# Matmuls of zeros put into TensorE's idle time at the LayerNorm boundaries of a two-part transformer block

## The chip, the cores and the metric

The kernel runs on one core of one Trainium2 chip. A core has TensorE (PE in the profile, with PEld for its weight loads), VectorE (DVE), ScalarE (ACT), GpSimd (POOL) and SyncE (SP, which here only issues DMAs). The metric is the device time of one execution in microseconds; lower is better.

## The reference

One sequence of 256 tokens with 1024 features passes through two blocks of two layers each. What surrounds the change is the first block:

```python
h = layer_norm(x, ln_in_g, ln_in_b)
for l in range(DEPTH):                       # DEPTH = 2
    proj = h @ w_in[l]                       # 1024 -> 1888
    ...                                      # conv branch, GQA, gated spatial unit, MLA
    mix = jnp.concatenate([o_a, o_b, o_c, o_d], axis=-1) @ w_out[l]
    h = layer_norm(DEEPNORM_ALPHA * h + mix, ln_mix_g[l], ln_mix_b[l])
    up = depthwise_conv(h @ ffn_w_up[l], ffn_conv_w[l], ffn_conv_b[l])
    f = (jax.nn.silu(up[..., :D_FF]) * up[..., D_FF:]) @ ffn_w_down[l]
    h = layer_norm(DEEPNORM_ALPHA * h + f, ln_ffn_g[l], ln_ffn_b[l])
```

The second block has four feed-forward parts, a state-space mixer, a sliding-window attention and two cross-attentions, each behind an RMS norm. All numbers are float32.

## The kernel before, in words

The program is written by hand, one instruction stream for each engine, with semaphores between them; each stream runs in the order in which its code stands. A list of phases (`phases()`) is the same for all engines: start, then for each layer of the first block `mixer`, `norm("mix", l)`, `convffn`, `norm("ffn", l)`, and then the second block.

Matmuls are made from split operands: a float32 number is a high part in a short format plus a low remainder, and three products (high by high, low by high, high by low; `PASSES`) stand for one. Weights come in units of 1 MB by DMA into a ring of three slots (`raw`); ACT writes the high parts (`w_hi`, L1193), DVE the low parts (`w_lo`, L1655). `feature_major` (L639) makes 128 output features by 256 tokens from 8 blocks of 128 input features: 24 matmuls of 256 columns. Two such halves are one weight unit (`pair_fm`, or `up_pair` in the feed-forward), so two units are 96 matmuls.

A LayerNorm boundary of the first block goes like this. The last projection before it adds into PSUM banks 4 to 7: banks 4 and 5 are the first 128 tokens (`tt` = 0), 6 and 7 the second 128. DVE adds them to the stream `x` (L1652), takes the statistics (L1730, L1732), ACT the square root (L1285), and DVE writes the centred and scaled rows to `z`, which lies in the tensor `mix` (L1738), and signals `z_ready` once for each `tt`. PE then transposes them in `turn` (L677), 8 blocks of 128x128 for each `tt`, into banks 0 to 3. ACT applies gain and bias to two blocks for each bank (L1221) and signals `xhi_ready`, four times in all. DVE has one piece of work between: the low part of a weight unit (L1655, 128x2048). Then, for each of the four banks, DVE writes `xt_hi` (L1718) and `xt_lo` (L1655) and signals `bank_drained`. The first matmul of the next phase (`stream_tile`, inside `feature_major`) waits for the first of these four parts, the matmuls of blocks 2, 4 and 6 for the others. POOL meanwhile makes the new `x` from `z` (L2298, L2299) with operations on the same 1024 columns.

`zero` is a tensor of 512 columns of bfloat16 zeros. Before the change it is used once in each feed-forward part: four matmuls of one row by 512 columns (L786) clear banks 4 to 7.

In the second block a boundary is an RMS norm; its `turn` is the same function.

Of the kernel before, what the change touches and what calls it, by code (L numbers as in the profile page):

```python
# [28 lines left out]
P = 128  # L29
# [253 lines left out]
def mixed_block_kernel(nc, inp, consts, mem_dram, out, upto=None):  # L283
# [6 lines left out]
    with ExitStack() as ctx:  # L290
        def sb(name, shape, dt=F32):
            return ctx.enter_context(nc.sbuf_tensor(name, shape, dt))

        def sem(name):
            return ctx.enter_context(nc.semaphore(name))

        bank = [ctx.enter_context(nc.psum_tensor(f"bank{b}", [P, HALF], F32)) for b in range(8)]
# [10 lines left out]
        mix = sb("mix", [P, 2 * KT, T])  # L308
        xt_raw = mix[:, 0:KT, :]
        z = mix[:, KT:2 * KT, :].rearrange("p (t a) b -> p t (a b)", t=TT)  # L310
# [14 lines left out]
        zero = sb("zero", [P, HALF], mybir.dt.bfloat16)  # L325
# [116 lines left out]
        xhi_ready = sem("xhi_ready")  # L442
# [56 lines left out]
        RESIDUAL = {("mix_norm_2", l): (f"ffn1.{l}", 0.5) for l in range(2)}  # L499
# [84 lines left out]
        def _(pe):  # L584
            seen = Count()
            mm = pe.matmul

            def claim(b, name):

                n = names.claim(b, name)  # L590
                if n >= 2:
                    pe.wait_ge(bank_drained[b], n - 1)
                return bank[b]

            def taken(name):

                b, n = names.of[name]
                pe.wait_ge(bank_drained[b], n)
# [53 lines left out]
            def pair_fm(unit, b, name):  # L652

                w = weights(unit, (KT, 256))
                dst = claim(b, name)
                first = First()
                for j in range(2):
                    ins = feature_major(dst[:, T * j:T * j + T], w, P * j, P, first)
                ins.then_inc(bank_full[b], 1)

            def pair_tm(unit, b, name):

                w = weights(unit, (KT, 256))
                dst = claim(b, name)
                first = First()
                for tt in range(TT):
                    ins = token_major(dst[:, 256 * tt:256 * tt + 256], w, tt, 0, 256, first)
                ins.then_inc(bank_full[b], 1)

            def turn(src, tag):  # L670

                for b in range(4):
                    claim(b, f"{tag}.t{b}")
                for tt in range(TT):
                    pe.wait_ge(z_ready, seen.next(z_ready))
                    for k in range(KT):
                        ins = pe.transpose(bank[k // 2][:, T * (k % 2) + P * tt:T * (k % 2) + P * tt + P],  # L677
                                           src[:, tt, P * k:P * k + P], ident)
                        if tt == TT - 1 and k % 2:
                            ins.then_inc(bank_full[k // 2], 1)  # L680

            def turned(tag):

                assert not stream_due
                stream_due.extend((2 * b, f"{tag}.t{b}") for b in range(4))
# [30 lines left out]
            def start():  # L716
                pe.wait_ge(ident_in, 16)
                pe.wait_ge(ready, 1)

                def turn_parameters(b, first, groups):  # L720
                    claim(b, f"par{first}")
                    for i, g in enumerate(groups):
                        ins = pe.transpose(bank[b][:, P * i:P * i + P], stage[:, g, :], ident)
                    ins.then_inc(bank_full[b], 1)

                pe.wait_ge(early_in, 16 * EARLY_DMAS)
                turn_parameters(0, 0, range(1))
                turn(memx, "mem")
                turned("mem")
                for j in range(4):  # L730
                    pair_fm(f"mem{j}", j % 2, f"memk{j}")
                for j in range(4):
                    pair_tm(f"mem{4 + j}", 2 + j % 2, f"memv{j}")
                    if j == 0:
                        pe.wait_ge(const_in, 16)
                    if j < 3:
                        mean_squares("mem", x_sq, j)
                pe.wait_ge(stage_in, 16 * STAGE_DMAS)
                turn_parameters(0, 1, range(1, 5))
                turn_parameters(1, 5, range(5, ngroups))  # L740
                mean_squares("mem", x_sq, 3)
                turn(z, "x0")

            def mean_squares(tag, sq, h):

                pe.wait_ge(sq_ready, seen.next(sq_ready))
                b = 4 + h % 2
                claim(b, f"{tag}.ms{h}")
                for c in range(2):
                    ins = mm(bank[b][:, 0:T], cst("mean256"), sq[:, 2 * h + c, :], start=c == 0, stop=c == 1)  # L750
                ins.then_inc(bank_full[b], 1)

            def norm(tag, l):
                if (tag, l) != ("ffn", 1):
                    turn(z, f"{tag}{l}")

            def ffn_any(tag, prev):

# [396 lines left out]
            def xattn(l):  # L1155
                turned(f"xattn_norm_2{l}")

                for j in range(4):
                    pair_fm(f"xq{l}.{j}", j % 2, f"xq{l}.{j}")
                    if j >= 1:  # L1160
# [4 lines left out]
                out_rows([f"xo{l}.{j}" for j in range(4)], f"xo{l}")  # L1165

            run(dict(start=start, mixer=mixer, norm=norm, convffn=convffn, ffn=ffn, ssd=ssd, swa=swa,
                     xattn=xattn, store=lambda: None))

# [461 lines left out]
        def _(dve):  # L1631
# [39 lines left out]
            def split():  # L1671

                q = split_next[0]
                split_next[0] += 1
                slot, _, _, n = split_waits(q)
                dve.wait_ge(hi_ready, q + 1)
                tt_(w_lo[:, q % RING, 0:n], raw[:, slot, 0:n], w_hi[:, q % RING, 0:n].bitcast(F32),
                    ALU.subtract).then_inc(unit_split, 1)
# [728 lines left out]
        def _(sp):  # L2407
# [63 lines left out]
            def stream_ffn(tag, w_up, w_down):  # L2471
                up = w_up.rearrange("(k p) n -> p k n", p=P)
                down = w_down.rearrange("(r p) n -> p r n", p=P)
                _, s0, _, q0 = place[f"{tag}.gate0"]
                columns(f"{tag}.gate0", w_up, 0, 256)
                columns(f"{tag}.up0", w_up, DFF, 256)

                def load(k, i, dst_rows, src):
                    s = (s0 + k) % RING
                    sp.wait_ge(unit_split, q0 + k - RING + 1 if i is None else i * 6 + q0 + k - RING + 1)  # L2480
                    sp.dma_start(raw[:, s, :].rearrange("p (a b) -> p a b", a=dst_rows), src).then_inc(landed[s], 16)

                with sp.Fori(0, TURNS, 1) as i:
                    for c in (1, 2):
                        k = 2 + 3 * (c - 1)
                        load(k, i, KT, up[:, :, bass.ds(i * 512 + 256 * c, 256)])
                        load(k + 1, i, KT, up[:, :, bass.ds(i * 512 + DFF + 256 * c, 256)])
                        load(k + 2, i, 2, down[:, bass.ds(i * 4 + 2 * (c - 1), 2), :])
                rows(f"{tag}.down{NCHUNK - 1}", w_down, CHUNK_F * (NCHUNK - 1))
# [74 lines left out]
```

## Time and profile before

| | us |
|---|---|
| median of 3 runs | 2071.95 |
| lowest, highest | 2069.97, 2077.83 |
| span of the profiled execution (all that is listed of its time) | 2080.7 |
| mean granted TensorE clock in it | 0.933 |
| PE busy | 1932.7 (93%) |
| DVE busy | 1285.5 (62%) |
| ACT busy | 892.0 (43%) |

The profile is one execution. The share of PE in the chain of work that ended last is 84%, of DVE 10%. The granted clock is a share of TensorE's full rate; it has two values in this trace, 1.00 (2.4 GHz) and 0.50 (1.2 GHz). In the views by window the columns are the stretch, its length, the busy time of each engine with the number of its instructions, the clock, and DMA. In the timeline the columns are start, duration, engine, line and operation, operands, shapes, count, and in brackets the idle time before with what ended it.

### The profile page before, as it was taken

What the parts mean: (1) busy time and instruction counts of PE and PEld (TensorE: products, weight loads), DVE (VectorE), ACT (ScalarE), POOL (GpSimd) and SP (SyncE); (2) the same over time, 40 slices, a digit from 0 to 9 for tenths busy, and PEclk for the clock granted to TensorE, in tenths of its full rate; (3) what the DMA queues carried; (4) which work ended last, traced back from release to release, by engine and by line L of the source; (5) the groups of instructions that cost most, each with busy time, mean ns of one, the idle gap of its engine ahead of it and who ended that gap; (6) DMA issues with size and microseconds to landing.
All of it is one profiled execution on the core that took longest, in us unless ns stands there. A gap on an engine that the chain in (4) does not pass through costs nothing.

```text
span 2080.7 us, 31025 instructions
## 1 busy us (share of the span) xinstructions
PE 1932.7 (93%) x12412; PEld 1724.3 (83%) x12412; DVE 1285.5 (62%) x1559; ACT 892.0 (43%) x1076; POOL 101.8 (5%) x79
## 2 busy tenths in 40 slices
PE   7989799978979997999988999999999988999999
PEld 7966699976679997998986788999899875688998
DVE  5786877777687776555646556555555557565555
ACT  5444444434444443334543354333433444444332
POOL 0300200020020000000041000000000000000000
PEclk9987899988889998999986999999999995899999
DMA  9531355542135554555531434555455430224553
GB/s 299 186 111 50 134 182 181 183 133 102 61 122 182 188 189 131 185 190 168 161 105 61 142 142 151 189 185 181 162 182 182 164 119 21 100 87 160 187 189 126
DMA packets 226642, 310.78 MB, mean 149 GB/s; under 512 B 6598, under 2 KB 199398, under 8 KB 225926
## 3 DMA queue, kind: packets, MB, share of 16 engines
q1 hardware_dynamic: 223750, 298.06, 42.4%
q0 software_dynamic: 2528, 10.14, 1.5%
q10 hardware_dynamic: 288, 1.52, 0.2%
q8 instruction: 53, 0.87, 0.2%
q14 instruction: 23, 0.19, 0.0%
HBM read 306.56 MB, written 3.15 MB: 149 GB/s over the span
## 4 chain that ended last, share of the span: by engine, by line
PE 84%; DVE 10%; ACT 3%; issue 1%; POOL 1%; DMA 0%; DVEq 0%; ACTq 0%
PE bank L639 47%; PE bank L799 17%; PE bank L709 7%; PE bank L648 3%; PE bank L864 2%; PE bank L836 2%; DVE w_lo L1655 2%; DVE work L1652 1%; DVE x L1652 1%; PE bank L850 1%; DVE work L1655 1%; ACT mix L1303 1%; PE bank L1108 1%; ACT w_hi L1193 1%; DVE work L2231 1%
## 5 line engine op out<-in xcount | busy, mean ns | idle before, releaser
L1655 DVE TENSOR_TENSOR w_lo<-raw,w_hi 128x2048 fp32r<-128x2048 f32 x280 | 646.3, 2312 | 513.2 <-ACT w_hi L1193 513.0
L1193 ACT ACTIVATE w_hi<-raw 128x2048 fp32r<-128x2048 f32 x280 | 533.2, 1905 | 813.0 <-PE bank L639 532.4
L639 PE MATMUL bank<-xt_hi,w_hi 128*128 128x256 f32 x2752 | 791.8, 288 | 37.0 <-DVE xt_lo L1655 24.9
L639 PE MATMUL bank<-xt_lo,w_hi 128*128 128x256 f32 x2752 | 785.8, 286 | 0.0
L639 PE MATMUL bank<-xt_hi,w_lo 128*128 128x256 f32 x2752 | 785.4, 285 | 0.0
L639 PEld LDWEIGHTS bank<-xt_hi,w_hi 128*128 128x128 f32 x2752 | 535.4, 195 | 47.0 <-DVE xt_lo L1655 17.0
L639 PEld LDWEIGHTS bank<-xt_lo,w_hi 128*128 128x128 f32 x2752 | 535.3, 195 | 3.1 <-issue 0.7
L639 PEld LDWEIGHTS bank<-xt_hi,w_lo 128*128 128x128 f32 x2752 | 534.9, 194 | 0.0
L799 PE MATMUL bank<-w_hi,act_hi 128*128 128x512 f32 x528 | 206.4, 391 | 0.0
L799 PE MATMUL bank<-w_lo,act_hi 128*128 128x512 f32 x528 | 206.2, 390 | 0.0
L799 PE MATMUL bank<-w_hi,act_lo 128*128 128x512 f32 x528 | 205.4, 389 | 0.0
L799 PEld LDWEIGHTS bank<-w_hi,act_lo 128*128 128x128 f32 x528 | 99.1, 188 | 21.1
L799 PEld LDWEIGHTS bank<-w_hi,act_hi 128*128 128x128 f32 x528 | 99.4, 188 | 19.8 <-DVE act_lo L1655 0.9
L799 PEld LDWEIGHTS bank<-w_lo,act_hi 128*128 128x128 f32 x528 | 99.4, 188 | 18.3
L1652 DVE SCALAR_TENSOR_TENSOR work<-bank,par,work 128x255 f32<-128x255 f32 (+2 forms) x212 | 92.4, 478 | 25.7 <-ACT work L1342 18.4
L1193 ACT ACTIVATE work<-bank 128x512 f32<-128x512 f32 (+6 forms) x96 | 51.5, 545 | 117.0 <-PE bank L850 56.3
L709 PE MATMUL bank<-w_hi,act_hi 128*128 128x512 f32 x224 | 89.5, 399 | 6.7 <-ACT work L1475 3.0
L709 PE MATMUL bank<-w_lo,act_hi 128*128 128x512 f32 x224 | 88.8, 397 | 0.0
L709 PE MATMUL bank<-w_hi,act_lo 128*128 128x512 f32 x224 | 88.7, 396 | 0.0
L836 PE MATMUL bank<-work 128*128 128x256 f32 (+3 forms) x192 | 64.5, 509 | 19.9 <-DVE work L1655 9.1
L1342 ACT ACTIVATE work<-bank,par 128x256 f32<-128x256 f32 x88 | 44.5, 555 | 64.6 <-PE bank L639 64.6
L677 PE MATMUL bank<-con,mix 128*128 128x128 f32 x192 | 34.2, 341 | 40.4 <-DVE mix L1824 26.0
(256 smaller groups left out, 1874.0 us busy)
## 6 DMA issues: line engine op xcount, KB each, us to landing
raw<-in_ffn_wi SPq DMA_DIRECT2D x88, 1024.0 KB, 5.0
raw<-in_ffn_w_up SPq DMA_DIRECT2D x44, 1024.0 KB, 5.1
raw<-in_ffn_wo SPq DMA_DIRECT2D x44, 1024.0 KB, 4.8
raw<-in_ffn_w_down SPq DMA_DIRECT2D x22, 1024.0 KB, 5.3
raw<-in_w_in SPq DMA_DIRECT2D x14, 1024.0 KB, 5.3
raw<-in_ssd_in_proj SPq DMA_DIRECT2D x14, 1024.0 KB, 5.1
raw<-in_mem_wkv SPq DMA_DIRECT2D x9, 1024.0 KB, 8.4
raw<-in_w_out SPq DMA_DIRECT2D x8, 1024.0 KB, 5.0
```

The source lines that it names most:

```text
L639: ins = first(mm(dst, w[s][:, k, c0:c0 + m], xt[v][:, k, :], start=k == 0 and p == 0, stop=k == KT - 1 and p == 2))
L648: ins = first(mm(dst, xt[s][:, k, P * tt:P * tt + P], w[v][:, k, c0:c0 + n], start=start and k == 0 and p == 0, stop=k == KT - 1 and p == 2))
L677: ins = pe.transpose(bank[k // 2][:, T * (k % 2) + P * tt:T * (k % 2) + P * tt + P], src[:, tt, P * k:P * k + P], ident)
L709: ins = first(mm(bank[b][:, :], act[s][:, u % 2, r, P * tt:P * tt + P], w[v][:, r, HALF * h:HALF * h + HALF], start=u == 0 and r == 0 and ...
L799: ins = first(mm(bank[b][:, :], act[s][:, c % 2, j, P * tt:P * tt + P], w[v][:, j, HALF * h:HALF * h + HALF], start=False, stop=True, skip ...
L836: ins = mm(bank[b][:, at:at + n], d["q"][t][c], d["k"][c][:, 0:n], start=c == 0, stop=c == len(d["k"]) - 1)
L850: ins = pe.transpose(bank[b][:, dst:dst + P], prob[:, h % prob.shape[1], d["at"][t] + P * s:d["at"][t] + P * s + P], ident)
L864: ins = mm(bank[b][r:r + m, T * c + q0:T * c + T], v[s], prob_t[:, h % 2, T * s:T * s + T - q0], start=s == 0, stop=s == TT - 1 or d["keys ...
L1193: return act.activation(dst, src, ACT.Copy)
L1342: ins = act.activation(dst[:, c % 2, j, :], bank[b][:, T * j:T * j + T], ACT.Identity, scale=par[:, cw, at], bias=par[:, cb, at])
L1652: return dve.scalar_tensor_tensor(out=out, in0=in0, scalar=scalar, in1=in1, op0=op0, op1=op1)
L1655: return dve.tensor_tensor(out=out, in0=in0, in1=in1, op=op)
```

## The change

A helper `fill(b, n)` issues n matmuls of one row of zeros, 128 columns of weights and 512 columns of moving data, into bank b, each with start and stop set, so that nothing reads what it writes. `norm` of the first block's boundaries now waits until banks 4 and 5 are drained, issues 8 fills, then calls `turn` with `filled=True`, which issues 4 fills behind the second wait for `z_ready` and ahead of the second 8 transposes; then come 6 fills, and 4 more behind each of the four signals of `xhi_ready`. All fills go to bank 4. That is 8 + 4 + 6 + 16 = 34 fills for a boundary. The boundaries are `("mix", 0)`, `("ffn", 0)` and `("mix", 1)`; for `("ffn", 1)` the function returns at once, as before. The other lines keep the count of `xhi_ready` right where PE doesn't wait for it.

```diff
-            def turn(src, tag):
+            def turn(src, tag, filled=False):
...
                 for tt in range(TT):
                     pe.wait_ge(z_ready, seen.next(z_ready))
+                    if filled and tt:
+                        fill(4, 4)
                     for k in range(KT):
...
+            def fill(b, n):
+
+                for _ in range(n):
+                    mm(bank[b][:, :], zero[0:1, 0:P], zero[0:1, :], start=True, stop=True)
+
             def norm(tag, l):
-                if (tag, l) != ("ffn", 1):
+                if (tag, l) == ("ffn", 1):
+                    return
+                if tag not in ("mix", "ffn"):
                     turn(z, f"{tag}{l}")
+                    seen.next(xhi_ready, 4)
+                    return
+                name = RESIDUAL[tag, l][0]
+                for h in range(2):
+                    taken(f"{name}.0{h}")
+                fill(4, 8)
+                turn(z, f"{tag}{l}", filled=True)
+                fill(4, 6)
+                for _ in range(4):
+                    pe.wait_ge(xhi_ready, seen.next(xhi_ready))
+                    fill(4, 4)
```

PE's stream of before at the boundary `("mix", 0)`, from the second 8 transposes' predecessor to the first product of the feed-forward:

```order
L709 MATMUL bank<-w_hi,act_lo 128x512
L677 MATMUL bank<-con,mix 128x128 [waits bank_drained3,bank_drained2,z_ready,bank_drained1,bank_drained0]
L677 MATMUL bank<-con,mix 128x128 x7
L677 MATMUL bank<-con,mix 128x128 [waits z_ready]
L677 MATMUL bank<-con,mix 128x128 x7
L639 MATMUL bank<-xt_hi,w_hi 128x256 [waits bank_drained0,unit_split]
```

The same place in PE's stream of the changed kernel (L760 is the fill, L679 the transposes):

```order
L760 MATMUL bank<-zero 128x512 [waits bank_drained5,bank_drained4]
L760 MATMUL bank<-zero 128x512 x7
L679 MATMUL bank<-con,mix 128x128 [waits bank_drained3,bank_drained2,z_ready,bank_drained1,bank_drained0]
L679 MATMUL bank<-con,mix 128x128 x7
L760 MATMUL bank<-zero 128x512 [waits z_ready]
L760 MATMUL bank<-zero 128x512 x3
L679 MATMUL bank<-con,mix 128x128 x8
L760 MATMUL bank<-zero 128x512 x6
L760 MATMUL bank<-zero 128x512 [waits xhi_ready]
L760 MATMUL bank<-zero 128x512 x3
```

The last two rows come four times in all, and behind them stands the same first product. The wait of the second transposes has moved to the fill ahead of them; 26 fills stand between the second `z_ready` and the first product, and 8 ahead of the first transposes. The streams of the other engines are as before.

## Rows read from the trace of the kernel before

**Rows 1.** The page's first line: span and instructions.

```profile
span 2080.7 us, 31025 instructions
```

**Rows 2.** The chain that ended last, boundary ("mix", 0): start, us, what.

```profile
214.95 2.94 DVE mix L1738
217.88 4.36 DVE w_lo L1655
222.24 2.49 DVE xt_hi L1718
...
224.75 2.72 DVE xt_lo L1655
...
227.61 13.71 PE bank L639 x96
241.32 0.96 PE bank L786 x4
242.28 11.71 PE bank L639 x96
```

**Rows 3.** The chain that ended last, behind the other two boundaries.

```profile
434.10 23.11 PE bank L639 x168
...
589.86 13.53 PE bank L639 x96
```

**Rows 4.** Busy time by window at ("mix", 0); the clock follows POOL's column.

```profile
211.54:214.95 3.41, 0.00 (x0) 0.00 (x0) 3.20 (x9) 0.29 (x1) 0.00 (x0) 1.00 0.00 0
214.95:217.94 2.99, 1.92 (x9) 1.55 (x9) 2.99 (x2) 0.00 (x0) 2.88 (x2) 0.51 0.00 0
217.94:219.91 1.97, 1.96 (x8) 1.56 (x8) 1.97 (x1) 1.25 (x3) 1.97 (x1) 0.50 0.00 0
219.91:227.60 7.69, 0.00 (x0) 0.02 (x1) 7.66 (x4) 2.51 (x6) 6.94 (x4) 0.50 0.39 136
227.61:232.00 4.39, 4.39 (x20) 4.39 (x21) 4.29 (x7) 1.91 (x1) 1.00 (x2) 0.50 0.59 218
```

**Rows 5.** The same view: the second transposes at ("ffn", 0) and ("mix", 1).

```profile
424.42:426.39 1.97, 1.97 (x8) 1.57 (x8) 1.97 (x1) 1.24 (x3) 1.97 (x1) 0.50 0.00 0
...
580.18:582.15 1.97, 1.97 (x8) 1.57 (x8) 1.97 (x1) 1.24 (x3) 1.97 (x1) 0.50 0.00 0
```

**Rows 6.** Timeline of the boundary ("mix", 0), PE, ACT and DVE.

```profile
217.94 1.97 PE L677 MATMUL bank<-con,mix 128*128 128x128 f32 x8 [1.04 <-DVE mix L1738]
218.66 3.76 ACT L1221 ACTIVATE mix<-bank,par 128x256 f32<-128x256 f32 x8 [4.37 <-PE bank L677]
...
227.39 0.41 DVE L1718 CAST xt_hi<-mix 128x512 fp32r<-128x512 f32 x1
...
228.45 0.42 DVE L1718 CAST xt_hi<-mix 128x512 fp32r<-128x512 f32 x1
```

**Rows 7.** Timeline: the zero matmuls that the kernel has already.

```profile
241.25 1.03 PE L786 MATMUL bank<-zero 1*128 1x512 bf16 x4
```

**Rows 8.** Timeline: matmuls of 512 columns at half clock, back to back.

```profile
1782.45 0.63 PE L709 MATMUL bank<-w_hi,act_lo 128*128 128x512 f32 x1
1782.87 0.63 PE L709 MATMUL bank<-w_hi,act_hi 128*128 128x512 f32 x1
```

**Rows 9.** Timeline and windows: matmuls of one row at L697, and after.

```profile
1777.96 3.67 PE L697 MATMUL bank<-wide,con 1*128 1x512 f32 x8 [0.52 <-issue]
...
1777.96:1781.70 3.74, 3.74 (x9) 1.52 (x10) 0.00 (x0) 0.00 (x0) 0.00 (x0) 1.00 0.00 0
1781.74:1785.10 3.36, 3.36 (x9) 2.58 (x10) 0.84 (x1) 1.91 (x1) 0.00 (x0) 0.50 0.00 0
```

**Rows 10.** Timeline and window: matmuls of 16 rows at L1093.

```profile
1107.97 4.51 PE L1093 MATMUL bank<-work,wide 16*128 16x256 f32 x11 [0.43 <-DVE work L1652]
...
1109.30:1112.70 3.40, 3.37 (x8) 1.87 (x7) 3.19 (x11) 1.00 (x3) 0.00 (x0) 0.50 0.62 252
```

**Rows 11.** Windows: 16 transposes of 128 rows at half clock, and after.

```profile
1884.10:1887.50 3.40, 3.36 (x16) 3.28 (x16) 2.98 (x3) 1.27 (x5) 0.00 (x0) 0.51 0.00 0
1887.50:1889.00 1.50, 0.67 (x6) 0.46 (x4) 1.50 (x5) 1.50 (x5) 0.00 (x0) 0.98 0.07 5
```

More of the change, by code:

```diff
@@ L742, in start @@
                 turn(z, "x0")
+                seen.next(xhi_ready, 4)
             def mean_squares(tag, sq, h):
@@ L751, in mean_squares @@
                 ins.then_inc(bank_full[b], 1)
+            def fill(b, n):
+                for _ in range(n):
+                    mm(bank[b][:, :], zero[0:1, 0:P], zero[0:1, :], start=True, stop=True)
             def norm(tag, l):
-                if (tag, l) != ("ffn", 1):
+                if (tag, l) == ("ffn", 1):
+                    return
+                if tag not in ("mix", "ffn"):
                     turn(z, f"{tag}{l}")
+                    seen.next(xhi_ready, 4)
+                    return
[8 more added lines that the diff above has]
+                    fill(4, 4)
             def ffn_any(tag, prev):
```

## The prediction

> **What bounds the kernel now.** I read the chain that ended last first. PE holds most of it: behind each boundary of the first block stand long pieces of L639, and between them at a boundary stand DVE pieces alone [rows 2, 3]. At ("mix", 0) the chain is: the second half of `z` on DVE (214.95, 2.94 us), the low part of a weight unit (4.36), `xt_hi` (2.49), `xt_lo` (2.72), and then PE from 227.61. So in a boundary DVE sets the end and PE waits; behind it PE sets the end again. A microsecond by which the first product starts later is a microsecond of the kernel, and a matmul behind it that gets faster is a gain, as long as its operands are there.
>
> Then the windows, for the clock [rows 4]. PE is idle from 211.54 to 214.95 with the clock still at 1.00; from 214.95 on it is 0.51, that is 1.2 GHz from the first transposes on. The second transposes run at 0.50, and so do the first 4.39 us of products. The other two boundaries are built alike: there too the second transposes run at 0.50 [rows 5].
>
> What half clock costs: two weight units (96 matmuls) take 11.71 us undisturbed, behind the boundary 13.71 [rows 2] and 13.53 [rows 3]: 2.0 and 1.8 us. At ("ffn", 0) 168 matmuls take 23.11 [rows 3] against 168 x 11.71/96 = 20.5: 2.6 us. Together 6.4 us, 0.3% of 2071.95, are all that the clock can give back at the three boundaries at which something is added. ("ffn", 1), the fourth, gets nothing.
>
> **What is added, and its price.** 34 fills at each of three boundaries, 102 in all. Their price depends on the clock. At full rate the four that the kernel has take 0.96 us in the chain [rows 2], 0.24 each, of the very form [rows 7]. At half rate the trace has none of them; the nearest row is a matmul of the same 512 columns with 128 rows, which starts each 0.42 to 0.43 us [rows 8]. I take 0.427. That it has other rows and another type doesn't matter if the columns set the pace; the lower end, full rate, is 0.24.
>
> *The first 8* begin when PE is done at about 211.5: 8 x 0.24 = 1.9 us in an idle time of 3.41 [rows 4]. Hidden, 1.5 us to spare. The wait for banks 4 and 5 costs nothing: DVE has drained these long before the last matmul, since it works on them while PE still fills banks 6 and 7.
>
> *The other 26* stand between the second `z_ready` and the first product. From the second transposes to the first product there are 227.61 - 217.94 = 9.67 us, at the other two 434.10 - 424.42 = 9.68 and 589.86 - 580.18 = 9.68 [rows 2, 3, 5]. The transposes take up to 1.97 of it [rows 6]; since that includes the tail of the last, 1.7 is what they hold up the next matmul. That leaves 7.7 to 8.0 us of cover.
> - At full clock: 26 x 0.24 = 6.2 us. Hidden, at least 1.5 us to spare.
> - At half clock: 26 x 0.427 = 11.1 us. They stick out by 3.1 to 3.4 us, and with 0.1 to 0.2 for the starts behind waits (four fills take 0.96 and not 4 x 0.216) by 3.3 us, which I take. The first product at ("mix", 0) would then start at 230.9.
>
> *The four fills ahead of the second transposes* delay these by 1.7 us at half clock. ACT, which began 0.72 us after them at 218.66 [rows 6], begins at 220.4 and has its first bank at 221.3; DVE turns to it at 222.24, when it is done with the weight unit [rows 2]. 0.9 us to spare. If that cover were gone DVE would be later, but it could be late by 3.3 us before the first product noticed, since PE is then still in its fills. The four waits for `xhi_ready` end by about 224.1, ahead of the fills behind them. Queued behind all this on PE is only the first product; for it wait ACT and DVE (the next weight unit) and, behind those, SP's loads. These all shift with it and keep their distance.
>
> **Which of the two clocks?** This decides. The fills have one active row of 128. The trace has one stretch in which PE does nothing but such work: 8 matmuls of 1x512 at L697, 3.67 us back to back, no gap, at clock 1.00; the next matmuls, products of 128 rows, find 0.50 [rows 9]. PE was 100% busy and the clock fell all the same. A second stretch, matmuls of 16 rows at L1093, runs from 1107.97 for 4.51 us; the clock is at 0.50 from 1109.3 on, with PE at work [rows 10]. The opposite, 16 transposes with all 128 rows, started at 0.51 and the products behind them found 0.98 [rows 11]. So what held or raised the clock here was work on many rows, and work on one row did not. I conclude that the 8 fills don't keep the clock, that it is half by the second `z_ready` as now, and that the 26 run at half rate.
>
> The Trainium skill ("TensorE: Matmul & The Clock Gate", the section "Why this matters for your kernels") says to leave no long idle gap between bursts of matmuls, or the clock drops, and says nothing of rows. By that rule the fills, which leave no long gap, would hold it; [rows 9] speak against it. What the rule would give is the first rival below.
>
> **Sum.** Three boundaries x 3.3 us = +9.9 us; the lower and upper ends of the overhang, 3.1 and 3.6, give +9.3 and +10.8. The products behind run at half clock for about as long as now (no gain), shifted, with up to a microsecond either way in each since the place at which the clock comes back need not be the same. Against its own execution: 2080.7 [rows 1] + 9.9 = 2090.6. The runs' median is 8.7 us below that span, and nothing in the sum depends on which of the two it is: 2071.95 + 9.9 = 2081.8 us, +0.48%.
>
> **Rivals.**
> *A. The fills hold the clock.* For it: PE would be idle for no more than 1.5 to 3 us at a time. Against: [rows 9]. Place: the products behind the boundary. Then nothing sticks out, and the 6.4 us of half clock are gained, less what DVE allows: the parts of `xt_lo` come 1.06 us apart (227.39, 228.45 [rows 6]), 6 matmuls at full clock need 6 x 0.12 = 0.72, so PE waits 3 x 0.34 = 1.0 at each boundary. Gain 6.4 - 3.0 = 3.4 us: 2068.5 us. It decides from the point at which the second transposes run at 1.00. This is the side on which the kernel isn't slower; even the whole 6.4 would be 0.3%.
> *B. The fills hold it for a while.* If the clock falls only in the last gap, with the fills done, they cost nothing and gain nothing: 2072.0. It would need one-row work to count for something. If it falls within the 26, anything from 0 to +9.9.
> *C. Late transposes become the bound.* If DVE had to wait for ACT by more than 3.3 us, the boundary would be longer than my sum; with 0.9 us of slack and 3.3 us more behind, ACT would have to be some 4 us late. Each further microsecond costs 3: at +1 us, 2084.8. Little speaks for it.
> *D. It doesn't do what it says.* It fills three boundaries, not four; that is in the sum. The fourth would add another 3.3 us or 1.
>
> **How the numbers follow.** Forecast 0.85, A 0.08, B 0.05, C 0.02. What a measurement of this kernel can tell from no change is about 0.5%, 10.4 us (the three runs lie 7.9 us apart). The forecast lies at +9.9, just inside; with its own ends of 9.3 to 10.8, a clock that comes back somewhat elsewhere and the scatter of medians, I give it 0.47 to lie beyond: 0.85 x 0.47 = 0.40, plus C, 0.41 slower. A and B lie within, and faster by over 0.5% exceeds even the whole 6.4 us: 0.03 for scatter. The likeliest one's own range is 2077 to 2087; the low end is taken down to 2073 to take in most of B.
>
> **What would show it.** In the changed kernel's profile: second transposes and the 26 fills at 0.50, fills 0.43 apart, first products about 13.0 us behind the second `z_ready` (9.7 now), with no idle time of PE before them; the 8 first fills at 1.00 inside the idle time. DVE's chain through the boundary as long as now. Wrong, if the windows from 215 to 227 us show 1.00 and PE idle ahead of the first product: then A. Wrong in size, if fills at half clock start closer than 0.43 apart, or if a later stage absorbs the shift.

## The result, and the profile after

The changed kernel takes 2083.40 us (median of 7 runs, 2082.05 to 2087.70) against 2072.01 for the kernel before (7 runs). The ratio is 1.0056 with a 95% interval of 1.0041 to 1.0071: slower, by 11.4 us on the medians. 2081.8 was forecast, with 2077 to 2087 as the range of the likeliest case.

The chain that ended last, at the same boundary ("mix", 0) as [rows 2] (start, us, what). Lines have moved: the fill is L760, the transposes L679, DVE's second half of `z` L1760.

```profile
210.23 2.95 DVE mix L1760
...
213.22 1.88 PE bank L760 x4
215.10 1.90 PE bank L679 x8
217.00 9.49 PE bank L760 x22
226.50 13.41 PE bank L639 x96
```

Before, three DVE pieces stood between `z` and the first product: 4.36, 2.49 and 2.72 us. In their place the chain now runs over PE: 4 fills, 8 transposes, 22 fills. From the second `z_ready` to the first product it was 9.67 us; now it is 226.50 - 213.22 = 13.28. DVE's own work ends in time, as the timeline of DVE shows (start, duration, engine, line): its fourth and last part of `xt_lo` is written from 225.25 on, before PE starts with the first.

```profile
213.08 4.43 DVE L1677 TENSOR_TENSOR w_lo<-raw,w_hi 128x2048 fp32r<-128x2048 f32 x1
...
222.68 0.41 DVE L1740 CAST xt_hi<-mix 128x512 fp32r<-128x512 f32 x1
...
225.25 0.69 DVE L1677 TENSOR_TENSOR xt_lo<-mix,xt_hi 128x512 fp32r<-128x512 f32 x1
```

The windows of the changed kernel, which answer to [rows 4]; the clock follows POOL's column.

```profile
206.75:210.26 3.51, 1.90 (x9) 0.69 (x9) 3.30 (x9) 0.33 (x2) 0.00 (x0) 0.94 0.00 0
210.26:213.22 2.96, 1.94 (x9) 1.55 (x9) 2.96 (x2) 0.00 (x0) 2.88 (x2) 0.50 0.00 0
213.22:215.03 1.81, 1.81 (x4) 0.42 (x4) 1.81 (x1) 0.00 (x0) 1.81 (x1) 0.50 0.00 0
...
217.00:226.50 9.50, 9.50 (x24) 3.05 (x23) 8.81 (x9) 2.52 (x6) 6.23 (x4) 0.50 0.59 191
226.50:230.30 3.80, 3.80 (x18) 3.80 (x19) 1.25 (x1) 1.91 (x1) 0.00 (x0) 0.50 0.22 78
230.40:239.80 9.40, 9.40 (x80) 9.30 (x78) 4.39 (x5) 2.82 (x3) 0.00 (x0) 1.00 0.35 112
```

The 8 fills lie in the idle time and cost nothing. They don't keep the clock: it is at 0.50 from the first transposes on. Then PE is 100% busy from 213.22 to 226.50 and the clock stays at 0.50 all the while; it comes back 3.8 us after the real products have begun. The other two boundaries are the same to 0.01 us: their 22 fills take 9.49 us each, and from the second `z_ready` to the first product there are 13.28 us.

```profile
426.80 9.49 PE bank L760 x22
436.30 22.86 PE bank L639 x168
...
581.53 9.49 PE bank L760 x22
591.02 13.71 PE bank L639 x96
```

Three times 13.28 - 9.68 is 10.8 us. The products behind, at half clock for a while, take 13.41, 22.86 and 13.71 against 13.71, 23.11 and 13.53 [rows 2, 3]: 0.4 less in all. So 10.4 us of the 11.4 are seen in these rows; the other 1.0 is less than the scatter of the runs (2069.97 to 2079.10 before).

The span of the profiled execution is 2081.3 us, only 0.6 above that of before [rows 1], and that misleads. The execution of before that was profiled was a long one for its kernel, by 8.7 us over the median. The first block's attentions show why. In the second of them the clock is at 0.50 for 34 us, in the first line (the kernel before), while the changed kernel has 1.00 for 6.5 us in the midst of the same stage.

```profile
505.20:539.20 34.00, 29.37 (x85) 15.78 (x86) 25.64 (x68) 9.96 (x30) 2.52 (x2) 0.50 0.13 47
```

```profile
507.00:523.80 16.80, 12.02 (x32) 6.89 (x32) 14.90 (x39) 6.08 (x18) 2.52 (x2) 0.50 0.28 98
524.10:530.60 6.50, 6.50 (x39) 3.40 (x38) 6.40 (x18) 2.08 (x7) 0.00 (x0) 1.00 0.01 3
530.90:537.40 6.50, 6.50 (x17) 4.19 (x17) 4.26 (x13) 1.51 (x5) 0.00 (x0) 0.50 0.00 1
```

Nothing was changed in that stage. Counted between the same two instructions of DVE, the two attentions take 65.0 and 52.6 us in the profile of before and 60.0 and 48.2 in this one: 9.4 us, which hide nearly all of the boundaries' 10.4. Where the clock comes back differs from execution to execution, and two profiles can't be compared by their spans; each boundary was compared by itself, and the kernels by their medians.

### The profile page after: what moved, and what is told of

Read it like the earlier page. It is cut to its first block, busy times and chain, and to the rows that moved or that the text cites. A ratio compares the mean times of both kernels' runs of the same rounds, so it can differ in the third digit from the quotient of the medians.

```text
span 2081.3 us, 31232 instructions
## 1 busy us (share of the span) xinstructions
PE 1959.1 (94%) x12514; PEld 1729.5 (83%) x12514; DVE 1285.8 (62%) x1559; ACT 892.6 (43%) x1076; POOL 101.8 (5%) x79
## 4 chain that ended last, share of the span: by engine, by line
PE 85%; DVE 9%; ACT 3%; issue 1%; POOL 1%; DMA 0%; DVEq 0%; ACTq 0%
PE bank L639 47%; PE bank L821 17%; PE bank L711 7%; PE bank L648 3%; PE bank L886 2%; PE bank L858 2%; PE bank L760 2%; DVE w_lo L1677 1%; DVE work L1674 1%; DVE x L1674 1%; PE bank L872 1%; DVE work L1677 1%; ACT mix L1325 1%; PE bank L1130 1%; ACT w_hi L1215 1%
## 5 line engine op out<-in xcount | busy, mean ns | idle before, releaser
L858 PEld LDWEIGHTS bank<-work 64*128 64x128 f32 (+2 forms) x192 | 40.0, 261 | 37.5 <-issue 12.5
```

Source lines behind the costliest of these rows:

```text
L858: ins = mm(bank[b][:, at:at + n], d["q"][t][c], d["k"][c][:, 0:n], start=c == 0, stop=c == len(d["k"]) - 1)
```

## The experiments

Theory R is that of the prediction: work on one row doesn't hold the clock, so the 26 fills run at half rate and are longer than the DVE work that would hide them. Its rivals: zeros don't count, whatever the rows (Z), and the added waits and instructions cost the time, whatever the clock (W).

**128 rows instead of one, `e1_rows128`.**

```diff
-                    mm(bank[b][:, :], zero[0:1, 0:P], zero[0:1, :], start=True, stop=True)
+                    mm(bank[b][:, :], zero[:, 0:P], zero[:, :], start=True, stop=True)
```

> The changed kernel with one edit: every fill has 128 rows of zeros instead of one; number, columns, bank and waits are the same. Theory R (rows decide: work on one row doesn't hold the clock, work on 128 rows does, zeros or not): the second transposes and the 26 fills run at 1.00, are done about 3 us before the first product is ready, nothing sticks out; the products behind the boundary run at 1.00 if the clock survives that last gap, so 2068 to 2072 us. Rival Z (zeros don't count, whatever the rows): as the changed kernel, 2083 us, second transposes at 0.50. Rival W (the added waits and instructions cost the time, not the clock): also 2083 us, whatever the clock shows.

Measured: 2070.18 us, ratio to the kernel before 0.9979 (0.9967 to 0.9992). Faster than before, and 13 us faster than the change, with the same number of instructions, waits and columns. The windows at ("mix", 0), from the second `z_ready` on:

```profile
214.85:215.72 0.87, 0.87 (x4) 0.44 (x5) 0.87 (x1) 0.00 (x0) 0.87 (x1) 1.00 0.00 0
215.72:216.80 1.08, 1.08 (x10) 0.96 (x9) 1.08 (x1) 0.66 (x2) 1.08 (x1) 1.00 0.00 0
216.80:221.40 4.60, 4.60 (x22) 1.96 (x20) 4.60 (x2) 3.10 (x7) 4.48 (x2) 1.00 0.12 32
221.40:224.60 3.20, 0.17 (x2) 0.09 (x1) 3.17 (x3) 0.00 (x0) 2.57 (x2) 1.00 0.69 282
224.60:229.30 4.70, 4.67 (x24) 4.44 (x25) 4.60 (x7) 1.91 (x1) 0.94 (x2) 0.64 0.69 220
```

Fills and transposes at 1.00, then 3 us of idle time, as forecast for this case. Here the clock falls behind that gap, in the last line, and this boundary gains nothing; its first 96 products are as long as before (13.6 us against 13.7). At ("ffn", 0) and ("mix", 1) it was not as expected: the clock had fallen by the second `z_ready`, the second transposes ran mostly at half rate, and then it rose. Two windows of the same kernel at ("ffn", 0), most of the second transposes, and the 22 fills with the gap behind them:

```profile
422.90:424.00 1.10, 1.10 (x7) 1.09 (x6) 1.10 (x1) 0.42 (x1) 1.02 (x2) 0.54 0.00 0
424.00:430.90 6.90, 5.18 (x26) 2.34 (x25) 6.87 (x4) 3.34 (x8) 6.23 (x3) 1.00 0.50 154
```

So zeros count when they go through all rows; Z and W are both ruled out. In this boundary the products are paced by DVE: its chain has DVE parts 1.06 to 1.08 us apart ahead of the last 90 matmuls, where without them PE alone would stand.

```profile
430.77 0.35 DVE xt_hi L1740
...
431.83 0.36 DVE xt_hi L1740
...
432.91 0.35 DVE xt_hi L1740
...
434.03 11.05 PE bank L639 x90
```

**Half the columns, `e3_cols256`.** The same 102 fills and all waits; the 26 of each boundary have 256 columns. One of the three places that the edit changes:

```diff
-                fill(4, 6)
+                fill(4, 6, 256)
```

> The changed kernel with the 26 fills behind the second z_ready of one row by 256 columns in place of 512; the same instructions, waits and order. Theory R: 26 x 0.213 = 5.5 us at half clock against 7.7 to 8.0 us of cover, so they are hidden and the time is that of the kernel before, 2072 us. Rival W: as the changed kernel, 2083 us. At 0.50 the second transposes in any case.

Measured: 2072.70 us, ratio 0.9985 (0.9970 to 1.0000), no change from before. The timeline at ("mix", 0) has the fills at half clock, done, and PE idle for 1.95 us ahead of the first product:

```profile
216.54 1.03 PE L760 MATMUL bank<-zero 1*128 1x256 bf16 x4 [1.15 <-DVE mix L1760]
217.50 1.97 PE L679 MATMUL bank<-con,mix 128*128 128x128 f32 x8
219.40 4.87 PE L760 MATMUL bank<-zero 1*128 1x256 bf16 x22
226.22 0.55 PE L639 MATMUL bank<-xt_hi,w_hi 128*128 128x256 f32 x1 [1.95 <-DVE xt_lo L1677]
```

With 22 fills in 4.9 us instead of 9.5 the cover is long enough. The price of the change is the columns that stick out. W is ruled out a second time.

**Only the first 8, `e2_first8`.**

```diff
-                    if filled and tt:
-                        fill(4, 4)
...
-                fill(4, 6)
-                for _ in range(4):
-                    pe.wait_ge(xhi_ready, seen.next(xhi_ready))
-                    fill(4, 4)
+                seen.next(xhi_ready, 4)
```

> Only the first 8 fills of one row, in PE's idle time ahead of the first transposes; the 26 behind the second z_ready and the waits for xhi_ready are gone. Theory R: 8 x 0.22 us are hidden in an idle time of 3.4 us and the clock falls as before: 2072 us, no change. A rival by which the first 8 hold the clock up to the second transposes would show these at 1.00 and give up to 3 us back.

Measured: 2072.12 us, ratio 0.9988 (0.9971 to 1.0005), no change. The clock falls before the second transposes.

This kernel is also the better yardstick for what a clock that is held or raised gives. Count each boundary between the same two instructions of DVE, from the second half of `z` to the low part of a later weight unit (214.95 to 261.56, 421.43 to 471.79 and 577.19 to 612.41 in the profile of before), and add the three:

| kernel | sum of the three stretches, us |
|---|---|
| before | 132.2 |
| the change | 142.6 |
| `e2_first8`, `e3_cols256`, `e12_swa_only` (clock half by the second `z_ready`, nothing sticks out) | 130.6, 130.4, 130.4 |
| `e1_rows128`, `e4_rows128_more` | 129.6, 130.0 |
| `e11_rows96`, `e7_swa` | 128.7, 128.7 |

The profile of before had the clock come back late at ("ffn", 0), so 1.6 to 1.8 us of what any fill seems to gain against it come without any work of the fills. Fills of 96 and 128 rows give 0.4 to 2 us at the three boundaries, not more; and against this yardstick the change costs 12.0 us, near the 11.4 of the medians.

**64, 32 and 96 rows, `e5_rows64`, `e6_rows32`, `e11_rows96`.** The edit is that of the first experiment, with `zero[0:64, ...]` and so on.

> The changed kernel with fills of 64 rows of zeros in place of one. Theory R, in the form that the active rows count in proportion: half the rows are between the row that fell (1) and the one that held (128), so either the second transposes run at 1.00 in most boundaries (2070 to 2073 us) or the 26 fills run at 0.50 throughout (2083 us); which of the two bounds how many rows are needed. A form of the theory in which any tile above one row is enough would give 2070 us.

> The changed kernel with fills of 32 rows of zeros. Theory R with rows in proportion: as one row, 0.50 at the second transposes and the fills, 2083 us. If one strip of 32 rows were the unit that counts, as 128 rows: 2070 us.

> The changed kernel with fills of 96 rows of zeros. Theory R: 64 rows fell and 128 held. Near 2070 us with the second transposes at 1.00 if 96 are enough, near 2083 us with the 26 fills at 0.50 if not.

| rows | us | ratio to before, interval |
|---|---|---|
| 1 (the change) | 2083.40 | 1.0056, 1.0041 to 1.0071 |
| 32 | 2083.50 | 1.0050, 1.0030 to 1.0070 |
| 64 | 2082.51 | 1.0037, 1.0021 to 1.0054 |
| 96 | 2069.95 | 0.9973, 0.9955 to 0.9992 |
| 128 | 2070.18 | 0.9979, 0.9967 to 0.9992 |

With 64 rows, PE 100% busy, the clock stays at 0.50 through the fills, as the window at ("mix", 0) shows. With 96 rows it had fallen by the second `z_ready` too, at all three boundaries, so the second transposes ran at 0.50, which the expectation had not allowed for; but then it came back. The timeline at ("ffn", 0) has 4 fills in 1.68 us and, behind the transposes, 22 in 4.91, where 64 rows take 9.56.

```profile
221.86:231.30 9.44, 9.44 (x23) 3.02 (x22) 8.83 (x9) 2.55 (x6) 6.25 (x4) 0.50 0.57 194
```

```profile
422.41 1.89 PE L760 MATMUL bank<-zero 96*128 96x512 bf16 x4 [1.89 <-DVE mix L1760]
424.09 1.81 PE L679 MATMUL bank<-con,mix 128*128 128x128 f32 x8
425.74 4.91 PE L760 MATMUL bank<-zero 96*128 96x512 bf16 x22
```

It isn't in small steps: the costs of 1, 32 and 64 rows can't be told apart by their intervals, nor the gains of 96 and 128.

**More fills of 128 rows, `e4_rows128_more`.** 12 more behind the last four, to close the last gap.

```diff
+                fill(4, 12)
```

> All fills with 128 rows, and 12 more behind the last four, so that at full clock they end some 0.4 us before the first product's operands are there. Theory R: the clock stays at 1.00 through the boundary, the products behind run at full rate and are paced by the xt_lo parts: 2068.5 us, 3.4 below the kernel before. Rival Z: 38 fills at half clock stick out by 3.6 + 12 x 0.427 = 8.7 us three times, 2098 us.

Measured: 2071.76 us, ratio 0.9987 (0.9972 to 1.0002). Not the 2068.5 that I expected, and 1.6 us above the first experiment. The chain at ("mix", 0) shows one reason why 2068.5 wasn't reached:

```profile
213.35 1.89 PE bank L760 x4
215.24 1.71 PE bank L679 x8
216.95 5.98 PE bank L760 x22
...
222.98 2.54 PE bank L760 x11
225.52 11.50 PE bank L639 x96
```

The products run at full rate at once, 11.50 for 96, but PE reaches them late, since the clock had fallen in the gap ahead of the second `z_ready` and part of the fills ran at half clock. What the clock gives back (11.50 against 13.71, 2.2 us) the fills take: 12.17 us from `z_ready` to the first product against 9.67, 2.5 us. A row of fills that just closes the gap at full rate has no room for a fall of the clock before it. At ("mix", 1) it was the same in part (10.93 us to the first product). At ("ffn", 0) the clock stayed at 1.00 throughout, as expected, and PE was idle for only 0.45 us ahead of the first product. These rows don't explain the 1.6 us, though: by the table above the three boundaries are 0.4 us longer than in the first experiment. What differs more in the two profiles is the second attention, 52.6 us here and 48.1 there, with nothing changed in it; this profile was of an execution of 2075.56 us, and six of the twelve runs lie at 2073.6 and above, six at 2069.9 and below. Whether the 12 fills have a part in that is open.

**The same in the sliding-window attention, `e7_swa`, `e12_swa_only`.** The trace of before has PE busy for 52.8 of 58 us at 0.50 there; its scores have 64 rows. Four fills go to the bank that the head's transposes will overwrite:

```diff
                     b = 2 + h % 2
-                    pe.wait_ge(prob_ready, seen.next(prob_ready))
                     claim(b, f"{tag}.p{h}")
+                    if tag == "w":
+                        fill(b, 4)
+                    pe.wait_ge(prob_ready, seen.next(prob_ready))
```

> Fills of 128 rows at the three boundaries and 4 more for each of the 16 heads of the sliding-window attention, ahead of the wait for the probabilities. There PE is busy almost all of 58 us at 0.50 in the kernel before, with scores of 64 rows. Theory R: the 64-row scores keep the clock down, the fills bring the mean of active rows up, and the stage runs at 1.00 for most of its time: up to 1 us less for each head, 2055 to 2065 us. Rival: the stage is bound by DVE and ACT at either clock, and the fills only add 16 x 4 x 0.22 to 0.43 us: 2070 to 2095 us.

> The kernel before, with no fill at any boundary and 4 fills of 128 rows for each head of the sliding-window attention. Theory R: the attention's part of the gain alone, 7 to 8 us: 2064 to 2066 us; the boundaries' 2 to 4 us are missing.

Measured: with the boundaries' fills 2062.31 us, ratio 0.9952 (0.9934 to 0.9970); with the attention's alone 2065.27, ratio 0.9947 (0.9926 to 0.9968). Both beat the kernel before and the change. The medians lie 3 us apart and the intervals overlap, so which is the better one isn't settled. The stage, before and in `e7_swa`:

```profile
1716.90:1774.90 58.00, 52.76 (x150) 29.59 (x151) 40.73 (x129) 27.43 (x101) 0.00 (x0) 0.50 0.05 17
```

```profile
1711.50:1759.00 47.50, 44.16 (x218) 24.60 (x218) 36.15 (x116) 24.49 (x88) 0.00 (x0) 1.00 0.00 1
```

64 more matmuls and a shorter stage, because everything in it runs at 1.00; for some 7 us ahead of it and 7 us behind it the clock is at 0.50. Between the same instructions of DVE (the first `rmax` of this attention, 1715.85, and the weight unit behind the matmuls of L697, 1784.26, in the profile of before) it is 68.4 us before, 59.8 in `e7_swa` and 62.0 in `e12_swa_only`, where the clock is at 0.50 for 6.8 us in the middle. In the other profiles without fills there it is 68.4 to 69.0.

**One row there, `e10_swa_row1`.** The edit: `fill(b, 4, 1)`, one row, in the attention only.

> Fills of 128 rows at the three boundaries and 4 of one row for each head of the sliding-window attention. Theory R: they don't hold the clock, the stage runs at 0.50 with 64 fills of 0.427 us on a PE that is nearly always busy there: 2070 + 27 less the idle time that they fill (some 5 us) = 2088 to 2097 us. A rival by which the gain of the 128-row fills came from anything but their rows (the claim ahead of the wait, for one) expects 2062 us.

Measured: 2105.10 us, ratio 1.0137 (1.0108 to 1.0167); 43 us more than with 128 rows, for the same instructions. I expected 2088 to 2097 and was 8 us short at least. The window says where: 94 us at 0.50 with PE busy for 93.5 of them.

```profile
1716.00:1810.00 94.00, 93.48 (x239) 43.83 (x238) 39.67 (x117) 26.27 (x89) 0.00 (x0) 0.50 0.00 1
```

The 58 us at half clock of before, less 5 us of idle PE that is filled, plus 64 x 0.427 = 27 make 80. What my expectation lacked is the work behind: before, the last heads and the one-row matmuls of L697 ran at 1.00 for 6.8 us, the line below and [rows 9]; at 0.50 that work takes twice as long, some 7 us more (an estimate from these 6.8).

```profile
1774.91:1777.90 2.99, 2.54 (x15) 1.51 (x13) 2.05 (x4) 1.39 (x4) 0.00 (x0) 1.00 0.00 0
```

Between the same two instructions as above it is 97.5 us against 68.4 before: 29, that is 22 + 7, of the 35 us by which this kernel is above the first experiment (2070.18). Of the other 6, the profiles show 3.5 in the first attention of the first block, 65.0 us against 61.5, where the two kernels are the same; the rest stays open.

**Two for each head, `e9_swa2`.**

> Fills of 128 rows at the three boundaries, and 2 in place of 4 for each head of the sliding-window attention. Theory R: if two are enough to hold 1.00 there, each head is 0.43 us shorter than with four, 16 x 0.43 = 7 us: 2055 us. If two aren't enough, the stage is at 0.50 and the fills cost 16 x 2 x 0.43 = 14 us on a busy PE: about 2083 us. The rival that the clock has no part in it expects a steady 2059 us.

Measured: 2069.07 us, ratio 0.9967 (0.9951 to 0.9982), but the runs spread from 2062.48 to 2070.14, and in the profile the stage has 13.4 us at 0.50 in its middle, with PE busy all the time:

```profile
1717.80:1734.70 16.90, 12.60 (x64) 6.88 (x64) 15.81 (x47) 8.87 (x33) 0.00 (x0) 1.00 0.00 0
1734.90:1748.30 13.40, 13.40 (x39) 6.95 (x38) 7.06 (x26) 5.97 (x25) 0.00 (x0) 0.50 0.01 1
```

Two fills are at the edge here; neither of the two cases expected came, but a mixture of both.

**Everywhere, `e8_all`.** Besides: `fill(4, 42)` at the fourth boundary, `fill(4, 16)` ahead of the first block's attentions, `fill(b, 4)` in each of their heads, `fill(b, 2)` ahead of each pair of 16-row matmuls in the state-space part.

> As the last, and fills of 128 rows also at the fourth boundary (42 in 10 us of idle time), ahead of the first block's attentions (16), ahead of the transposes of each of their heads (4) and with the 16-row matmuls of the state-space part (2 for each pair of heads). Theory R: the clock stays at 1.00 in more of these stages; each of them is shorter by what PE sets of it: 2045 to 2065 us. Rival: where the clock is at 0.50 anyway the fills stand on PE's path: 106 more fills, up to 45 us on top, 2070 to 2110 us.

Measured: 2074.34 us, ratio 1.0002 (0.9987 to 1.0018), 12 us worse than `e7_swa`. The rival was right for the state-space part. The clock is at 0.50 as before, for 47.6 us instead of 40.8, the kernel before first:

```profile
1109.40:1150.20 40.80, 32.19 (x113) 26.75 (x112) 27.26 (x60) 12.60 (x25) 0.00 (x0) 0.50 0.08 27
```

```profile
1101.20:1148.80 47.60, 39.49 (x127) 28.58 (x126) 27.98 (x62) 13.02 (x25) 0.00 (x0) 0.50 0.07 24
```

Elsewhere it was another thing. In each attention of the first block the clock was at 1.00 for longer, 10.2 us against 6.8 in `e7_swa`, and still each took 3.0 us more (63.0 and 51.2 us against 60.0 and 48.2, between the same instructions of DVE). Both lie within what this stage takes in the profiles of kernels with no fills in it, 59.9 to 65.1 and 48.0 to 52.6, so no gain is shown there and no cost either. At the fourth boundary the clock stayed at 1.00 up to the first products, and the stretch was only 0.3 us shorter. The state-space part, 84.6 us against 77.9, is a loss: in the profiles of kernels without fills there it is 77.6 to 78.3.

## Why the prediction was right

- **What bounds the boundary**: DVE before, with 7.7 to 8.0 us of idle PE behind it. Right: `e3_cols256` fits under this cover, the change doesn't.
- **The first 8 are hidden**: right, by `e2_first8` and by the window from 206.75.
- **Price of a fill at half clock, 0.427 us**: 9.49/22 = 0.431 in the chain. Right.
- **The overhang, 3.3 us for a boundary**: 3.60 measured, at each of the three. The 4 fills take 1.88, the transposes 1.90 and the 22 fills 9.49, 13.28 with the rounding; my sum had 1.7, 1.7, 9.4 and 0.15. The terms that were too small are the two at which PE goes from fills to transposes and back. From the first of the 4 fills to the first transpose there are 1.81 us, and from there to the next fill 1.90, at half clock, at all nine boundaries of the kernels with 1, 32 and 64 rows; with 96 and 128 rows it is 1.68 and 1.71 where the clock is at 0.50 throughout, which is what my sum had. So going between matmuls of few rows and of 128 costs 0.32 us for the pair; why isn't shown. Three times that is 1.0 of the 1.6 us between 2081.8 and 2083.4; the rest is within the scatter. That the forecast stood at +0.48% and the result at +0.56%, on the other side of the 0.5% that I had put at nearly even odds, is chance: the sum's own ends, +9.3 and +10.8 us, already lay on both sides of it.
- **ACT's slack of 0.9 us**: held. ACT began at 215.76 with its first of 8, 2.54 us behind `z_ready`, and DVE went from the weight unit to `xt_hi` without a wait (213.08 + 4.43, then 217.44). Rival C has no part in it.
- **Which clock**: 0.50 for all 78 fills that mattered. The one stretch at L697 [rows 9], supported by [rows 10], was the right thing to trust over the rule that a PE which is kept busy, without long gaps, keeps its clock. "TensorE: Matmul & The Clock Gate" of the Trainium skill has that rule under "Why this matters for your kernels"; here the trace doesn't agree: the change left PE no idle time at all for 13 us, at three places, and the clock didn't rise. With 96 and 128 rows in the same schedule it did rise.
- **Rival A**, priced at -3.4 us with a held clock: `e1_rows128` gives -4.4 by the ratio of 0.9979 (its interval is -1.7 to -6.8). That the two agree is in part luck. The clock was held through none of the three boundaries, and by the stretches between the same instructions they gave 2.6 us against the profile of before and 1.0 against `e2_first8`; of the rest, the kernel before had runs above 2080 us (2083.0 the longest beside this experiment) and this one none above 2073.7, for which no reason is shown. The pacing by DVE in it was right: 96 products take 12.4 us there, by the starts of the first and last, and 11.6 where nothing paces them.
- **The products behind, unchanged in their half clock**: right, 0.4 us less in three boundaries.

## What to carry to other kernels

Look at the active rows of work that is put in to hold or raise TensorE's clock, not only at its length: fills of 96 and 128 rows raised it here, those of 64 and fewer never did, and zeros served. Price such work at the half rate first, for that is what it costs if it fails, and ask whether it still fits into the wait that hides it. The most was gained where PE was busy at half clock with small matmuls, not idle: 7 to 9 us in one attention against 2 at most at three boundaries. That is no rule: in the state-space part the fills, two for each pair of heads, only cost time.

## What the runs showed of the hardware that I had not expected

- Columns don't make up for rows: 22 matmuls of 512 columns, 64 rows high, kept PE at 100% for 9.4 us and the clock stayed at 0.50; the same with 96 rows, begun at 0.50 as well, went on at 1.00. Between 64 and 96 rows the kernel's time has a step, and between 1 and 64 none that can be seen (2083.4, 2082.5 and 2070.0 us for 1, 64 and 96); nothing between 64 and 96 was tried.
- Zeros count. 128 rows of zeros raised the clock from 0.50 to 1.00 with nothing but transposes and themselves at work (`e1_rows128`, ("ffn", 0)). Since 16 transposes alone were followed by 1.00 as well [rows 11], it is the runs with 64 rows, the same transposes and no rise, that show the zeros' part.
- Going from fills of 1, 32 or 64 rows to transposes of 128 and back took 0.32 us more for the pair, at half clock, than with fills of 96 or 128 (1.81 and 1.90 us against 1.68 and 1.71).
- The kernel before scatters from 2069.5 to 2083.3 us over all runs made beside the experiments, and where the clock returns in a stage of small matmuls is a part of it: one attention had 34 us at 0.50 in one profile, and some 24 us in that of a kernel with the same instructions there.
